# Hybrid attention step on one core: prompt attention turned and done by head pairs, probabilities scaled on VectorE

## The reference, cut to what matters

```python
# MLA, per head: s = q_lat.ckv + q_rope.krope ; p = causal softmax ; o = p ckv, then w_uv
o_cmp = softmax(q . kc) vc            # 31 compressed blocks, mask by block end
o_sel = softmax(q_rot . k_sel) v_sel  # prompt: all 8 blocks are selected, so causal
o_win = softmax(q_rot . k_win) v_win  # window 512 = whole prompt, so causal
o_nsa = g0 * o_cmp + g1 * o_sel + g2 * o_win     # sigmoid gates per head
mixed = concat([o_mla * silu(z_mla), o_nsa * silu(z_nsa)], -1)
y = layer_norm(ALPHA * x + mixed @ w_o)
```

## Time and profile before

| | us |
|---|---|
| three timed runs, median (lowest to highest) | 582.52 (581.32 to 587.35) |
| the profiled execution's own time | 580.11 |
| its span, first to last instruction | 578.3 |
| TensorE busy | 511.3 |
| mean granted TensorE clock | 0.956 |

### The profile page before, as it was taken

How to read it: one execution, slowest core, us unless ns; L and a number is a source line. 1 busy time by engine, 2 the same in 40 slices (tenths; PEclk the granted TensorE clock), 3 DMA queues, 4 the chain that set the end, 5 groups by cost and what they waited for, 6 DMA issues and landing times. The chain is left out here.

```text
span 578.3 us, 9014 instructions
## 1 busy us (share of the span) xinstructions
PE 511.3 (88%) x2996; PEld 323.9 (56%) x2996; DVE 249.9 (43%) x678; ACT 169.4 (29%) x511; POOL 111.4 (19%) x192
## 2 busy tenths in 40 slices
PE   6969949999999899967999869988979979999984
PEld 3434436646555664556576647756558654646641
DVE  0041151330648723566356525564344461817315
ACT  0070001211113211235346323433723460605010
POOL 0043432236521333221000100010412210000000
PEclk9979969999999989969799989899989999999998
DMA  8975504452520905041137584420017010101001
GB/s 287 294 249 145 147 1 157 135 147 70 159 56 17 333 33 146 3 146 43 59 112 240 214 307 126 170 74 1 0 47 292 1 45 1 73 1 71 3 0 73
DMA packets 49160, 64.74 MB, mean 112 GB/s; under 512 B 10362, under 2 KB 39546, under 8 KB 49018
## 3 DMA queue, kind: packets, MB, share of 16 engines
q1 hardware_dynamic: 48218, 63.10, 33.6%
q0 software_dynamic: 512, 1.05, 0.7%
q10 hardware_dynamic: 384, 0.01, 0.0%
HBM read 59.89 MB, written 8.41 MB: 118 GB/s over the span
## 5 line engine op out<-in xcount | busy, mean ns | idle before, releaser
L845 PE MATMUL psum<-wring,bufA 128*128 128x512 f32 (+1 forms) x320 | 130.8, 564 | 0.0
L1361 ACT ACTIVATE wring<-wring,small 128x128 f32<-128x128 f32 (+3 forms) x96 | 53.9, 561 | 141.0 <-DVE small L1632 140.3
L845 PEld LDWEIGHTS psum<-wring,bufA 128*128 128x128 f32 x320 | 61.6, 195 | 59.0 <-issue 55.1
L1632 DVE CUSTOM_DVE_ANT_0 wring<-psum,const 128x128 f32<-128x128 f32 (+3 forms) x96 | 46.5, 486 | 76.5 <-PE psum L1054 65.0
L1257 PE MATMUL psum<-ring,comp 128*128 128x512 f32 x128 | 56.5, 595 | 1.5 <-issue 1.5
L1054 PE MATMUL psum<-mid,qrT 128*128 128x128 f32 (+3 forms) x128 | 52.3, 493 | 2.0 <-DVE small L1632 1.2
L815 PE MATMUL psum<-const,wring 128*128 128x128 f32 x248 | 46.6, 284 | 5.7 <-ACT wring L1438 4.0
L815 PEld LDWEIGHTS psum<-const,wring 128*128 128x128 f32 x248 | 32.6, 146 | 32.6 <-issue 18.8
L1085 PE MATMUL psum<-kv,wring 128*128 128x64 f32 x320 | 45.1, 273 | 3.2 <-DVE bufA L1660 1.8
L1085 PEld LDWEIGHTS psum<-kv,wring 128*128 128x128 f32 x320 | 42.9, 200 | 5.9 <-DVE bufA L1660 2.5
L1257 PEld LDWEIGHTS psum<-ring,comp 128*128 128x128 f32 x128 | 23.8, 190 | 28.9 <-issue 28.9
(11 more groups left out here) (233 smaller groups left out, 705.7 us busy)
## 6 DMA issues: line engine op xcount, KB each, us to landing
wring<-in_w_in SPq DMA_DIRECT2D x4, 2048.0 KB, 9.0
ring<-in_cmp_pages SPq DMA_DIRECT2D x64, 128.0 KB, 2.4
ring<-in_sel_pages SPq DMA_DIRECT2D x48, 128.0 KB, 2.3
ring<-in_mla_pages SPq DMA_DIRECT2D x40, 128.0 KB, 2.7
ring<-in_w_o SPq DMA_DIRECT2D x1, 4096.0 KB, 13.2
out_s_win<-in_state_win_kv SPq DMA_DIRECT2D x1, 4064.0 KB
ring<-in_win_pages SPq DMA_DIRECT2D x6, 512.0 KB, 5.7
bufA<-in_x_t SPq DMA_DIRECT2D x8, 272.0 KB, 5.5
```

The source lines that it names most:

```text
L845: ins = pe.matmul(bank[:, 0:w], xT[:, c, t * P:(t + 1) * P], wr[:, b % 2, c, 0:w], start=(c == 0), stop=(c == KC - 1))
L1361: ins = act.activation(Pp[:, n % 4, 0:w], Pp[:, n % 4, 0:w], ACT.Exp, bias=nmp[:, k, h:h + 1], scale=-1.0, accum_out=lp[:, k, h:h + 1])
L1632: ins = dve.tensor_tensor_reduce(Pp[:, n % 4, 0:w], bank[:, 0:w], mask, -(MLA_SCALE if kind == "pmla" else NSA_SCALE), CLAMP, ALU.add, ALU ...
```

## The change

The units become head pairs, one head of each group (x, g = 0, 1): per tile one pcmp unit of all eight heads, 4 psel, 4 pwin and 4 pmla units, 52 in all. Scores of psel and pwin use the 64 rows of their own group (no padK), the two heads of a pair in two banks; pools A and S are one pool of four banks. The probabilities are scaled by gate/sum before they are turned, in a new step pnorm one slot after the score, on VectorE. The value product has V stationary (64 columns) and the turned probabilities moving; its output is features by tokens, the heads of a pair in the two halves of the partitions, and the three NSA branches add up in one bank; a tile's output is one product with z on VectorE (`tile_out`). The gates are projected in that layout too (`gate_columns`: weights stationary, 512 tokens moving), with columns of w_in and rows of w_o reordered on the host, so the prompt needs no transposes ahead of the output projection. GpSimd's sums, padK and mixT for the prompt are gone. The blocks' order is now MLA, Q, CMPSEL, WINGATE, ZNSA, ZMLA; the first 18 units (tiles 0 and 1) are woven into ZMLA, the other 18 NSA units into decode. There, a score is followed at once by new and min, and Ps has two buffers. pmla and the output go from tile 3 down to tile 0; four vup steps stand in item sel 1.

```diff
-BLK = [(CUTS[0], CUTS[3] - CUTS[0]), (CUTS[4], MW), (CUTS[5], 2 * KVW), (CUTS[3], MW),
-       (CUTS[7], KVW + 3 * H), (CUTS[9], MW)]
-B_MLA, B_Q, B_CMPSEL, B_ZMLA, B_WINGATE, B_ZNSA = range(6)
+BLK = [(CUTS[0], CUTS[3] - CUTS[0]), (CUTS[4], MW), (CUTS[5], 2 * KVW), (CUTS[7], KVW + 3 * H), (CUTS[9], MW),
+       (CUTS[3], MW)]
+B_MLA, B_Q, B_CMPSEL, B_WINGATE, B_ZNSA, B_ZMLA = range(6)
+GATES = (B_ZNSA, B_ZMLA)
...
-UNITS = ([(i, kind, h) for i in range(PT) for kind in KINDS[:3] for h in range(G if kind == "pcmp" else H)]
-         + [(i, "pmla", h) for i in range(PT) for h in range(H)])
-NU, N_NSA = len(UNITS), len(UNITS) - PT * H
-BRANCHES = []
+UNITS = ([(i, kind, x) for i in range(PT) for kind, n in (("pcmp", 1), ("psel", HG), ("pwin", HG)) for x in range(n)]
+         + [(i, "pmla", x) for i in reversed(range(PT)) for x in range(H // 2)])
+NU, N_NSA = len(UNITS), len(UNITS) - PT * H // 2
+PAIRS = [0]
 for _u in UNITS:
-    if _u[:2] not in BRANCHES:
-        BRANCHES.append(_u[:2])
-T_LAG, V_LAG = 3, 5
-ORDER = [ST] + list(range(PT))
+    PAIRS.append(PAIRS[-1] + int(_u[1] != "pcmp"))
+T_LAG, V_LAG = 3, 4
+N_EARLY = 18
+ORDER = [ST] + list(reversed(range(PT)))
...
+        elif halved(b, t):
+            products.append(([("zpre", b, t)], 3.4))
+            products.append(([("proj", b, t)] + now, 3.4))
+        else:
+            products.append(([("proj", b, t)] + now, 3.7 if t == PT else 6.8 * BLK[b][1] / 512))
...
-    products[-3:-3] = [([("pad", 0)], 0), ([("pad", 1)], 0)]
-    steps += weave(products[first:], cmp + [([], 30)])
-
-
-    s = [([("qhead",)], 1), ([("qlat",)], 1.5), ([("zrecip", *seq[-1])], .5)]
+    gates = len(products) - 2 * PT - 1
+    steps += weave(products[first:gates], cmp + [([], 6)])
...
+        if 0 <= m - 1 < NU:
+            now.append(("pnorm", m - 1))
...
+    def cost(m):
+        i, kind, _ = UNITS[min(m, NU - 1)]
+        return 0.6 if kind == "pcmp" else 0.65 * (i + 1) + 0.2
+
+    p = [(slot(m), cost(m)) for m in range(N_NSA)]
+    steps += weave(products[gates:], p[:N_EARLY])
...
+        body = [([("score", *x), ("new", *x), ("min", *x)], SCORE_US[x[0]] + 1)]
...
-    A = Uses(2, 0, STEPS, a_uses)
-    S = Uses(2, 2, STEPS, s_uses)
+    A = Uses(4, 0, STEPS, a_uses)
...
+            def gate_columns(b, c, half):
+                if c == 0 and half == 0:
+                    pe.wait_ge(w_in[b % 2], 16 * ((b + 1) // 2))
+                pool, u = product(b, c)
+                bank = claim(pool, u) if half == 0 else bank_of(pool, u)
+                for k in range(half * KC // 2, (half + 1) * KC // 2):
+                    ins = pe.matmul(bank, wr[:, b % 2, k, c * P:(c + 1) * P], xT[:, k, 0:SEQ],
+                                    start=(k == 0), stop=(k == KC - 1))
+                if half == 1:
+                    ins.then_inc(pool.full[u % pool.n], 1)
...
+                for g in range(G):
+                    bank = claim(A, u + g)
+                    if kind == "pmla":
+                        h = 2 * x + g
+                        ins = pe.matmul(bank[:, 0:keys], QT[:, i % 2, h, :], KT[:, h, 0:keys], start=True, stop=True)
+                    else:
+                        d, kT = slice(g * HD, (g + 1) * HD), selKT if kind == "psel" else winKT
+                        ins = pe.matmul(bank[:, 0:keys], qrT3[d, x, q], kT[d, 0:keys], start=True, stop=True)
+                    ins.then_inc(A.full[(u + g) % A.n], 1)
...
-                        ins = pe.matmul(bank[:, h * HD:(h + 1) * HD], PTp[:, n % 4, j * P:(j + 1) * P], v,
-                                        start=(j == 0), stop=(j == i))
-                if n + 1 == NU or UNITS[n + 1][:2] != (i, kind):
+                        at = (j * G + g) * P
+                        ins = pe.matmul(bank[g * HD:(g + 1) * HD, x * P:(x + 1) * P], v, PTp[:, n % 2, at:at + P],
+                                        start=(kind == "pmla" and x == 0 and j == 0), stop=(last_of_tile(n) and j == i))
+                if last_of_tile(n):
...
+            def gate_of(i, kind):
+
+                b = KINDS.index(kind)
+                return gate3[:, i, b * H:(b + 1) * H].rearrange("p (g x) -> p x g", g=G)
+
+            def norm_unit(n):
+                i, kind, x = UNITS[n]
+                dve.wait_ge(p_exp, n + 1)
+                c = coef[:, n % 4, :]
+                if kind == "pcmp":
+                    p = Pp[:, n % 4, 0, 0:H * CHP].rearrange("p (h n) -> p h n", h=H)
+                    ok(dve.tensor_reduce(c, p, AX_X, ALU.add))
+                    ok(dve.tensor_scalar(c, c, 1e-30, None, ALU.max))
+                    ok(dve.reciprocal(c, c))
+                    cg = c.rearrange("p (x g) -> p x g", x=HG)
+                    ok(dve.tensor_tensor(cg, cg, gate_of(i, kind), ALU.mult))
+                    dve.tensor_tensor(p, p, c.unsqueeze(2).broadcast_to([P, H, CHP]), ALU.mult).then_inc(p_norm0, 1)
+                    return
+                dve.reciprocal(c[:, 0:G], lp[:, n % 4, 0:G]).then_inc(p_coef, 1)
+                dve.wait_ge(p_coef, PAIRS[n + 1])
+                for g in range(G):
+                    p = Pp[:, n % 4, g, 0:(i + 1) * P]
+                    if kind == "pmla":
+                        ins = dve.tensor_scalar(p, p, c[:, g:g + 1], None, ALU.mult)
+                    else:
+                        ins = dve.tensor_scalar(p, p, c[:, g:g + 1], gate_of(i, kind)[:, x, g:g + 1], ALU.mult, ALU.mult)
+                ins.then_inc(p_norm0, 1)
+
...
+            def tile_out(i, kind):
+
+                k = 0 if kind == "pmla" else 1
+                dve.wait_ge(z_done, (2 - k) * NT)
                 pool, u = value_bank(i, kind)
-                bank = heads(arrive(pool, u))
-
-                ok(dve.tensor_scalar(coef, lp[:, k, :], 1e-30, None, ALU.max))
-                ok(dve.reciprocal(coef, coef))
-                if kind != "pmla":
-                    ok(dve.tensor_tensor(coef, coef, gate3[:, i, b * H:(b + 1) * H], ALU.mult))
-                dst = acc if kind == "pcmp" else otmp
-
-                sums = m - (m + 2) // 3 if kind != "pmla" else 2 * PT
-                if kind == "pcmp" and i:
-                    dve.wait_ge(mixed_n, i)
-                elif sums:
-                    dve.wait_ge(summed, sums)
-                dve.tensor_tensor(heads(dst), bank, coef.unsqueeze(2).broadcast_to([P, H, HD]), ALU.mult).then_inc(
-                    pool.free[u % pool.n], 1)
-
-                if kind == "pmla":
-                    wait_copied(dve, pool, u)
-                    z = zs[:, i, 0:MW]
-                    dve.tensor_tensor(z, z, otmp, ALU.mult).then_inc(mixed_m, 1)
+                z = zT[:, 4 * k:4 * k + 4, i * P:(i + 1) * P]
+                dve.tensor_tensor(z, four(arrive(pool, u), P), z, ALU.mult).then_inc(pool.free[u % pool.n], 1)
...
+                if step[0] == "bd":
+                    block_diagonal()
...
-                if step[0] == "branch" and step[2] in ("psel", "pwin"):
-
-                    i, kind = step[1:]
-                    bank, u = value_bank(i, kind)
-                    wait_copied(pool, bank, u)
-                    n = 2 * i + 1 + int(kind == "pwin")
-                    pool.tensor_tensor(acc, acc, otmp, ALU.add).then_inc(summed, 1)
-                    pool.wait_ge(summed, n)
-                    if kind == "pwin":
-                        z = zs[:, i, MW:]
-                        pool.tensor_tensor(z, z, acc, ALU.mult).then_inc(mixed_n, 1)
-                        pool.wait_ge(mixed_n, i + 1)
```

More of the change, by code:

```diff
@@ L235, in plan @@
             body.append(([("omla",)], 1))
+        if x == ("sel", 1):
+            body += [([("vup", t)], .9) for t in range(PT)]
         if x == ITEMS[-1]:
@@ L258, in cost @@
[L258 to L267 removed]
+    steps += weave(s, p[N_EARLY:])
     for m in range(N_NSA, NU + V_LAG):
         steps += slot(m)
[L272 to L280 removed]
@@ L292, in a_uses, with halved @@
+        steps += [step for step, at in OUT_AT.items() if at == m - N_NSA]
+    steps += [("root", PT - 1), ("out", PT, 0), ("norm_y", PT - 1), ("out", PT, 1), ("root", PT), ("norm_y", PT)]
+    return steps
+def halved(b, t):
+    return b == B_ZMLA and t < PT
 def a_uses(kind, *a):
@@ L1037, in scores @@
                     for hh in range(HG):
[L1038 to L1044 removed]
+                        ins = pe.matmul(bank[:, hh * G * CHP:(hh + 1) * G * CHP], qnT3[:, hh, q], kcbd,
+                                        start=True, stop=True)
@@ L1045, in scores @@
+                    ins.then_inc(A.full[u % A.n], 1)
+                    return
+                if kind == "pmla" and x == 0:
+                    for j in range(2):
+                        wait_copied(pe, T, T.at("qh", i, j=j))
+                    if i == PT - 1:
                         for j in range(HG):
-                            wait_copied(pe, S, S.at("kup", j))
+                            wait_copied(pe, A, A.at("kup", j))
                         pe.wait_ge(key_rows, 2)
```

(45 more changed lines are left out.)

560 lines of the change are left out of this document (285 added, 275 removed).

## The result

| | before | after |
|---|---|---|
| median of four runs | 581.92 us (579.94 to 587.35) | 593.03 us (592.20 to 597.69) |
| the profiled execution | 580.11, span 578.3, clock 0.956 | 592.20, span 590.4, clock 0.914 |

The ratio is 1.019 (95% interval 1.011 to 1.028): slower by about 11 us, where 555 us and a chance of 0.05 for slower stood in the prediction. In some executions of the kernels of experiments 2, 3 and 7 the core ran slower, at a lower granted clock: ratios here leave those out, medians do not, and the profiles of these three show such an execution.

A forecast was written before the change was run, and what follows sets the result against it. TensorE's in-order work, and whatever holds it up, was taken as the bound. Stages 215 + 61 + 140 + 135 = 551 us of span, plus 1.8: 553 against 580.1 profiled, 555 from the median of 582.5; range 530 to 575.

The forecast's parts named there:

- (7): Order of work: 18 of 36 NSA slots move ahead into the ZMLA gate block; stages then sum to 551 us.
- stage A: Work up to ZMLA: 244.5 us less the ZMLA block's 29.7 gives 215.
- (6): GpSimd loses branch sums and padK; each scaling meeting its instructions costs about 1 us, 5 us charged.
- Stage B: ZMLA with tiles 0 and 1: 56 us plus 5 for GpSimd = 61 (bounds 56 and 75).
- Stage C: Decode with tiles 2 and 3: about 105 us of TensorE work, page waits of 25, ending at 140.
- The floor before the first window score: In decode, SyncE's queue lets that score start no earlier than 35.5 + 47.4 = 83 us into the stage.
- 54% of 105 less 5: TensorE work left in decode after 83 us; with 5 us of latencies the stage ends at 140.
- The rival of the clock: A mean granted clock of 0.8 in the gate and decode stages adds 12 + 13 us: 580, no change; chance 0.1.
- Stage D: Prompt MLA, output projection and tail: 142.9 us less 4 for values and 3.5 for turns gives 135.
- The terms of TensorE's work: NSA pairs save 20 us, MLA pairs 4, pcmp 3, dropped turns of mixed rows 3.5: 30 us less.
- The rival of row halves that don't: Row halves of psel and pwin scores don't run side by side: +17 us of TensorE work, 567 us; chance 0.2.
- the line drawn through the earlier trace: VectorE scalings priced between 770 ns (1056 columns) and 254 (64): 0.49 to 0.29 us for 512 to 128 columns.

The follow-up runs named there:

- experiment 2: The kernel before, with only GpSimd's gathers of the rope pages moved early: 583.05 us, ratio 0.996.
- experiment 3: The kernel before, with only the block order changed (WINGATE projected ahead of ZMLA, plus a ScalarE wait): 597.01 us, ratio 1.014.
- experiment 7: The fastest kernel, with the first window pages issued ahead of the second 32 page numbers: 566.44 us, ratio 0.967.
- experiment 1: The changed kernel, with only GpSimd's 16 gathers of rope keys issued earlier, ahead of the CMPSEL ropes: 575.89 us, ratio 0.987.
- experiment 5: On top of experiment 1, 9 instead of 18 prompt attention slots beside the gate block: 563.53 us, ratio 0.964.
- experiment 9: Throwaway products in the two page waits: 16 or 8 each on experiment 1, 582.95 and 574.94 us; fewer on the fastest kernel, 558.28 and 556.73.
- the fastest kernel: The changed kernel with gathers early, no prompt units beside the gate block and the window copy behind the last decode loads: 556.29 us, ratio 0.952.

## Why the prediction was wrong

**The failed step is (7) with the line on stage A**, 244.5 less the ZMLA block = 215. It took that block out as if it were only its own work. What GpSimd did beneath it was put at nothing: 27 us of gathers, which this block had covered, and a wait of 16.60 us for TensorE once it was gone. (6) did look at GpSimd, but at its total (19% busy, "nobody's bound") and at what it loses; both were right and did not matter. Its list of what GpSimd still holds, "only SiLU products, ropes and copies", leaves the gathers out. The trace of before had it all: the gathers from 131 to 157, the first WINGATE rope at 198. With the gathers early A ends at 209.9, 5 us under the forecast; in after at 229.6. The price is about 17 us (experiments 1 and 2), which alone undoes most of the 27 forecast.

**Stage B** took 61.5 us for 61, in part by luck. TensorE's work was right (56.3 for 56). The 5 us put on top were charged for scalings that meet GpSimd; three pairs of scalings met a GpSimd instruction and took 1.5 us more for it in all (see VectorE below). Of the 5.2 us that TensorE idled, 4.8 were waits for ScalarE's copies of turned probabilities (L1424, 3.59 us the longest).

**Stage C, 19 us too low, in two terms.** The floor before the first window score was right in kind and 5 us short: 35.5 + 47.4 let the first selection page start as soon as SyncE is free, and left out that the pages wait for their slots too, 6.6 us in after. The earlier trace rows had that wait: SyncE was free at 279.97 and the first page went out at 295.74, after the 15.6 us shown above. Behind it, 57 us were forecast and 71 measured. "54% of 105 less 5" gave 52 us of work at full clock; it was 60.1 at 0.87, and if all of that clock's loss fell on work (13% of the stage's 71 us is 9), 51. The allowance of 5 us for latencies met 10.9. So the count of work was about right, and the slow clock and the waits of the decode chain were left out. Of the short waits, 2.80 us <-DVE L1646 and 2.39 <-DVE L1833 are the largest. The rival of the clock (a mean of 0.8 in B and C) came true in small: 0.94 and 0.86. How far this stage could be quicker at full clock stays open: experiment 9 raised the clock only inside the waits.

**That the moved slots buy nothing in C** was forecast ("that part of the 30 us and of the moved slots buys nothing"), and experiment 5 shows it. What the forecast did not ask is whether the move then harms: 9 slots fewer early give 12 us.

**Stage D** fell by 2.8 us, not 7.9. The work fell as forecast (TensorE busy 120.0 for 126.3 in the earlier trace rows, 6.3 for 7.5), but its idling rose from 8.7 to 12.2 us: TensorE waited 12.1 us for the copies of turned probabilities (6.9 for ScalarE's, L1424, and 5.2 for VectorE's, L1735), where before it waited 4.6 for them. That a pair with turn, copy and value in a row leaves less time for the copy fits this and was not tested.

**The terms of TensorE's work were right.** One slot of an NSA pair of i=3, from the chain of waits of after (start, us, what; score, turn, value):

```profile
430.97 1.06 PE psum L1098 x4
432.03 1.02 PE psum L843 x8
433.06 1.02 PE psum L1143 x16
434.08 1.07 PE psum L1261 x2
```

From start to start 1.06 + 1.03 + 1.02 = 3.11 us, for 3.02 forecast. Four score instructions of 512 columns would take 1.71 one after another at the earlier trace rows's 0.107 per 128 columns: the row halves do run side by side (0.86 and a switch), and so do the value products (0.054 each and a switch). The rival of row halves that don't falls. By these differences a switch costs 0.15 to 0.20, an estimate. TensorE's busy time fell by 20.5 us in after, at its lower clock; in the fastest kernel, at nearly before's clock (0.952 for 0.956), by 32.4, for 30 forecast.

**VectorE.** Busy 273.9, for "some 280". By form, the mean durations of the scalings are 14 to 44% over the line drawn through the earlier trace rows (0.49, 0.42, 0.35 and 0.29 us for 512 to 128 columns), within the bounds of 0.25 and 0.77, and those of 256 columns are above those of 384:

```profile
L1728 DVE TENSOR_SCALAR wring<-wring,small,gate 128x256 f32<-128x256 f32 x16 | 7.4, 503 | 0.3
L1728 DVE TENSOR_SCALAR wring<-wring,small,gate 128x384 f32<-128x384 f32 x16 | 7.0, 477 | 0.3
```

The two scalings of a pair overlap, and from the timeline a pair with nothing beside it takes 1.00, 0.87, 0.73 and 0.60 us for 512 to 128 columns, where twice the line gives 0.98, 0.84, 0.70 and 0.58. So the line was right. Beyond the overlap, the means are raised by the pairs that run beside an instruction of GpSimd: of the eight with 256 columns three (1.14, 1.15 and 1.42 us) and of those with 128 one (1.26), each beside a SiLU product; of those with 512 two (1.24 and 1.43), beside its copies and a rope; of those with 384 none. Two of the eight with 256, and what GpSimd did, from the timelines of VectorE and GpSimd in after:

```profile
271.06 0.73 DVE L1728 TENSOR_SCALAR wring<-wring,small,gate 128x256 f32<-128x256 f32 x2
277.19 1.14 DVE L1728 TENSOR_SCALAR wring<-wring,small,gate 128x256 f32<-128x256 f32 x2
```

```profile
276.59 1.27 POOL L1954 TENSOR_TENSOR zsil<-zsil,rtmp 128x512 f32<-128x512 f32 x1 [13.94 <-DVE rtmp L1783]
```

Such a meeting cost 0.2 to 0.7 us, where (6) took 1.

**The sum.** A kernel with the forecast's time exists, but it is not the kernel that was forecast: it has the gathers early, no slots beside the gates and the copy last. A ends at 211.0 (215), B takes 30.7 (61) and C 171.3 (140), together 202.0 (201), D and its tail 140.2 (135), 553.2 in all for 551, and 556.29 us for 555. That the sums agree is luck: B's 30 us too few stand against C's 31 too many, and D's 5 too many against A's 4 too few. Of the 37 us between it and after, experiment 1 gave 17, the slots back behind the gates and the copy the other 20.

## What to carry to other kernels

When an edit reorders blocks, write down for each engine queue what it issues between the block's neighbours, and where its next result is wanted: a block of work on one engine is also the cover of whatever another engine issues in that time. Total busy time doesn't show this; the order on the queue does: before, the first WINGATE rope was wanted 41 us after the last gather; after, 13 us before that gather was through (168.2 less 16.6 is 151.6, against 164.7). And where the pages of a stage arrive at a nearly fixed distance behind its start (87 to 93 us in the turned kernels), work moved ahead of it is work taken out of a wait; leave it in.

## What was not expected of the hardware

Sixteen gathers issued from GpSimd kept its queue for 27 us: 0.95 us each, 0.3 apart, and pauses of up to 5.75 us. Scalings of 256 columns took longer in the mean (503 ns) than those of 384 (477 ns), because three of their eight pairs ran beside a GpSimd instruction; undisturbed, a pair took 0.73 us against 0.87. And throwaway products raised the mean clock in all four kernels that had them (0.930 to 0.939 and 0.952 to 0.961 where they fit the waits), without making the kernel faster in any.
